# Moving the large tiles and the weight rings to SBUF addresses that are multiples of 2048 bytes, in a two-layer streaming encoder

## What is computed

```python
h = rmsnorm(x, norm_mix[l])
p = h @ w_in[l]                                   # 2048 -> 4608: q, k, v, pooling and conv inputs
y_b = diff_attention(q, k, v, lam, lam_init, diff_head_gain[l])
y_a = multiscale_pool(a_in, pool_w[l], pool_scale[l])
y_c = conformer_conv(c_in, ...)                   # GLU, causal depthwise conv 31, LayerNorm, swish, pointwise
x = x + jnp.concatenate([y_b, y_a, y_c], axis=-1) @ w_out[l]
h = rmsnorm(x, norm_ffn[l])
gu = h @ w_ffn_in[l]                              # 2048 -> 2 x 5504
g = causal_dwconv(gu[..., :D_FF], ffn_conv_w[l], ffn_conv_b[l])
x = x + (jax.nn.silu(g) * gu[..., D_FF:]) @ w_ffn_out[l]   # 5504 -> 2048
```

## The kernel before

| tile | bytes | start before | start after | before mod 2048 | after mod 2048 |
|---|---|---|---|---|---|
| x | 16384 | 16512 | 40960 | 128 | 0 |
| xg | 32768 | 32896 | 57344 | 128 | 0 |
| raw | 16384 | 65664 | 90112 | 128 | 0 |
| whi | 16384 | 82048 | 106496 | 128 | 0 |
| wlo | 16384 | 98432 | 122880 | 128 | 0 |
| con | 2304 | 114816 | 16512 | 128 | 128 |
| half | 4096 | 125088 | 26784 | 160 | 160 |
| gt | 4128 | 129184 | 30880 | 160 | 160 |
| y | 4096 | 133312 | 35008 | 192 | 192 |
| mix, hidden | 32768, 88064 | 137408 | 139264 | 192 | 0 |
| qT, kT, v | 8192 each | 170176 on | 172032 on | 192 | 0 |
| glu | 4576 | 194752 | 196608 | 192 | 0 |
| pw_sb, E, att and the rest | | 199328 on | 201184 on | 672 | 480 |

## Time and profile before

### The profile page before, as it was taken

The page is one execution under the profiler, slowest core; times in us unless marked ns, Lnnn a source line. Parts: engine busy times, 40 slices in busy tenths (PEclk is TensorE's granted clock), DMA queues, the critical chain, the costliest instruction groups (busy, mean ns, idle before and its releaser), DMA issues.

```text
span 2200.1 us, 35784 instructions
## 1 busy us (share of the span) xinstructions
PE 2109.1 (96%) x11874; PEld 1825.4 (83%) x11874; DVE 1522.1 (69%) x1941; ACT 1072.9 (49%) x1504; POOL 354.9 (16%) x315
## 2 busy tenths in 40 slices
PE   7769999999999999999997799999999999999997
PEld 6658888888888888888885588888888888888886
DVE  7898677766666666555479976876676666655555
ACT  5325754555555554443362366545554555544433
POOL 5692023000000000110119621220000000001110
PEclk9999999999999999999999899999999999999999
DMA  7334455555655565556563344555555555555553
GB/s 250 129 106 155 142 172 183 192 191 179 199 188 188 180 200 189 182 177 208 193 203 116 132 147 134 178 193 191 191 191 191 181 192 190 191 192 191 189 191 136
DMA packets 108534, 391.80 MB, mean 178 GB/s; under 512 B 12176, under 2 KB 12688, under 8 KB 108176
## 3 DMA queue, kind: packets, MB, share of 16 engines
q1 hardware_dynamic: 107136, 386.98, 53.4%
q10 hardware_dynamic: 1296, 3.55, 0.5%
HBM read 388.38 MB, written 2.10 MB: 177 GB/s over the span
## 4 chain that ended last, share of the span: by engine, by line
PE 85%; issue 6%; DVE 6%; POOL 1%; ACT 1%; DVEq 0%; DMA 0%; SPq 0%; POOLq 0%; ACTq 0%
PE bank L1134 54%; PE bank L1135 27%; DVE gt L711 3%; PE bank L1203 2%; DVE wlo L666 1%; PE bank L1192 1%; PE bank L1194 1%; PE bank L1193 1%; POOL ssq L1038 0%; POOL sq L1035 0%; PE bank L1253 0%; ACT whi L374 0%; DMA x<-xT 0%; DVE x L1013 0%; DVE x L875 0%
## 5 line engine op out<-in xcount | busy, mean ns | idle before, releaser
L666 DVE TENSOR_TENSOR wlo<-raw,whi 128x1024 fp32r<-128x1024 f32 x728 | 945.3, 1306 | 610.8 <-ACT whi L374 609.7
L1134 PE MATMUL bank<-xg,whi 128*128 128x512 f32 x3648 | 1293.7, 399 | 68.0 <-DVE wlo L666 24.8
L374 ACT ACTIVATE whi<-raw 128x1024 fp32r<-128x1024 f32 x728 | 763.5, 1056 | 806.1 <-PE bank L1135 727.7
L1135 PE MATMUL bank<-xg,wlo 128*128 128x256 f32 x3648 | 1025.8, 281 | 0.0
L1134 PEld LDWEIGHTS bank<-xg,whi 128*128 128x128 f32 x3648 | 692.5, 190 | 235.0 <-DVE wlo L666 23.8
L1135 PEld LDWEIGHTS bank<-xg,wlo 128*128 128x128 f32 x3648 | 696.9, 191 | 0.2
L1134 PE MATMUL bank<-hidden,whi 128*128 128x512 f32 x1376 | 484.6, 395 | 0.3
L1135 PE MATMUL bank<-hidden,wlo 128*128 128x256 f32 x1376 | 387.5, 282 | 0.0
L1134 PEld LDWEIGHTS bank<-hidden,whi 128*128 128x128 f32 x1376 | 258.8, 188 | 62.9 <-DVE wlo L666 1.6
L1135 PEld LDWEIGHTS bank<-hidden,wlo 128*128 128x128 f32 x1376 | 258.5, 188 | 0.0
L1134 PE MATMUL bank<-mix,whi 128*128 128x512 f32 x512 | 182.3, 398 | 0.4 <-DVE mix L837 0.4
(11 more groups left out here) (144 smaller groups left out, 1115.5 us busy)
## 6 DMA issues: line engine op xcount, KB each, us to landing
raw<-wstream SPq DMA_DIRECT2D x729, 512.0 KB, 3.4
pw_sb<-pww ACTq DMA_DIRECT2D x2, 1024.0 KB, 5.8
x<-xT SPq DMA_DIRECT2D x3, 512.0 KB, 9.0
outT<-x SPq DMA_DIRECT2D x6, 256.0 KB, 2.1
x<-xT SPq DMA_DIRECT2D x2, 256.0 KB, 4.3
raw<-wstream SPq DMA_DIRECT2D x2, 256.0 KB, 4.5
poolw_sb<-poolw ACTq DMA_DIRECT2D x2, 256.0 KB, 3.7
outT<-x SPq DMA_DIRECT2D x1, 512.0 KB, 3.0
```

Of the source, the lines that this page charges most:

```text
L374: nc.scalar.activation(whi[:, s, :], raw[:, s, :], ACT.Copy).then_inc(hi_ready, 1)
L666: nc.vector.tensor_tensor(wlo[:, s, :], raw[:, s, :], whi[:, s, :], ALU.subtract).then_inc(lo_ready, 1)
L1134: nc.tensor.matmul(ps[bank][:], whi[:, s, blk * P:blk * P + P], mov, start=first, stop=False)
L1135: return nc.tensor.matmul(ps[bank][:, 0:S], wlo[:, s, blk * P:blk * P + P], mov[:, 0:S], start=False, stop=last)
```

## The change

The declarations of the five large tiles move behind the small ones, and a tile of 464 floats that nothing uses fills the gap to the next multiple of 2048. The operations of every engine are the same, in the same order (3389 rows of TensorE's program, 1205 of VectorE's, 814 of ScalarE's, 344 of GpSimd's and 30 of SyncE's before and after): nothing but addresses changes. In the changed file lines stand 4 lower: L1134 becomes L1138.

```diff
+FILLER = 464
 ...
-        x = sb("x", [P, KC, S])
-        xg = sb("xg", [P, KC, 2 * S], f32r)
-        raw = sb("raw", [P, RING, PIECE])
-        whi = sb("whi", [P, RING, PIECE], f32r)
-        wlo = sb("wlo", [P, RING, PIECE], f32r)
         con = sb("con", [P, NCON])
         par = sb("par", [P, NPAR + 1])
 ...
         gt = sb("gt", [P, NT, S + 2])
         y = sb("y", [P, NT, S])
+        sb("filler", [P, FILLER])
+
+        x = sb("x", [P, KC, S])
+        xg = sb("xg", [P, KC, 2 * S], f32r)
+        raw = sb("raw", [P, RING, PIECE])
+        whi = sb("whi", [P, RING, PIECE], f32r)
+        wlo = sb("wlo", [P, RING, PIECE], f32r)

         with ExitStack() as mixers:
             mix = sb("mix", [P, KC, 2 * S], f32r, mixers)
```

## The result

The changed kernel takes 2217.5 us (median of 4, 2209.9 to 2221.5), the kernel before 2200.8 in the same series (4 runs, 2198.72 to 2202.6). The ratio is 1.0074, 95% interval 1.0056 to 1.0091: slower by 0.74%. The forecast was 2195.5, in a range of 2187 to 2203. The profiled execution took 2216.8 us with a span of 2215.0 us, 14.9 us more than the span of before.

What follows compares the result with a forecast made beforehand. TensorE's matmuls were taken to bound the kernel. 3.9 us gained over `hidden` less 0.6 lost in stage C gave 3.3 us: 2195.9 from the median 2199.18, stated as 2195.5, range 2187 to 2203.

Steps and rivals of the forecast that it cites:

- What bounds the kernel: Whole span: TensorE, its matmuls busy 96% of it, sets the time; the last-ending chain runs over TensorE for 85%.
- Pace goes with the distance to the rings: TensorE pairs: distance by 2048 between moving tile and weight rings sets the pace; `xg` at 0, slower `mix` and `hidden` at 64.
- The rival that addresses do nothing: Whole kernel: pace may go with place in SBUF or stage, not remainder; 2199, within 2 us; chance 0.27.
- Pairs over `hidden`: Stage D, 1376 pairs: `hidden` takes `xg`'s two levels; 3.9 us gained, 0.3 at worst, 6.9 at best.
- odds of 7 in 15: Two restarts a layer over `hidden`: odds of the slow level, 0.3533, leaving 3.0 us lost.
- Pairs over `mix`: Stage B, 512 pairs near 0.3533: nothing booked; 1.4 us a layer gained if a long run is drawn fast.
- the 47 pairs behind them: First 47 pairs of stage C in each layer: run on slow behind `mix`, 0.6 us lost.
- The cycles above the column count: 64 of 832 cycles in each pair might vanish: tens of microseconds; chance 0.02 within the 0.13 case without a slow level.
- The float32 matmuls of the earlier trace then reset the level to fast for the 1326 pairs behind them.: Stage C: plain float32 matmuls of 256 columns lead to 0.3467, as in 6 of 6 restarts; no loss booked.
- booked nothing for `xg`: Pairs over `xg`: tile and rings move together, their distance by 2048 stays 0, so 0 us.
- slow level in stage C: Rival: the reset ends at 0.3533, 8.8 us lost a layer; 2205 for one layer, 2214 for both; chance 0.10.

Runs made afterwards that it cites:

- experiment 4: Kernel before with rings moved by 2016 bytes: `xg` 32 bytes off the rings, `mix` 96, `hidden` 128; 2197.2 us, ratio 0.9983.
- experiment 7: Kernel before with small tiles and 1952 bytes put between `xg` and the rings: `xg`, `mix`, `hidden` all at distance 32; 2191.05 us, ratio 0.9947.
- experiment 8: Kernel before with rings moved by 2016 bytes: `xg` 32 bytes off the rings, `mix` 0, `hidden` 160; 2193.28 us, ratio 0.9958.
- experiment 14: Changed kernel with the rings ahead of `x` and `xg`: `xg`, `mix`, `hidden` 32 bytes off the rings, `con` still at 128; 2191.78 us, ratio 0.9956.
- experiment 9: Kernel before with all small tiles 128 bytes higher, large tiles at their old remainders; 2210.03 us, ratio 1.0048.
- experiment 10: Kernel before with `con` alone 128 bytes higher, all other tiles at their old remainders; 2202.79 us, ratio 1.0015.
- experiment 12: Changed kernel with all small tiles 256 bytes from the rings in place of 128; 2200.77 us, ratio 0.9994 against the kernel before.
- experiment 13: Changed kernel with `con` declared behind the other small tiles, at distance 0 from the rings; 2198.74 us, ratio 0.9992 against the kernel before.
- experiment 2: Kernel before with a gap of 1984 bytes putting `mix` and `hidden` at distance 0 from the rings; 2200.29 us, ratio 0.9988.
- experiment 3: Kernel before with a gap of 1984 bytes putting `hidden` alone at distance 0 from the rings; 2201.03 us, ratio 0.9993.
- experiment 5: Changed kernel's order of declarations with the filler 32 floats longer, large tiles at remainder 128 by 2048; 2197.62 us, ratio 0.9981 against the kernel before.
- experiment 6: Kernel before with everything shifted by 1920 bytes, so that `xg` and the rings start on multiples of 2048; 2202.2 us, ratio 1.0001.
- experiment 11: Kernel before with `ssq` and the small tiles behind it 128 bytes higher, `con` and `par` as before; 2200.8 us, ratio 0.9998.
- experiment 1: Changed kernel with `mix` and `hidden` back at distance 64 from the rings; 2218.96 us, ratio 1.007 against the kernel before.

## Why the prediction was wrong

**What bounds the kernel**: right. No engine but TensorE changed its time, and the changes of its pace and clock account for the span to a few tenths of a microsecond.

**Pace goes with the distance to the rings**: right, and shown by experiments 4, 7, 8 and 14, on three tiles and at several places. `hidden` lost its level of 0.3489 as forecast and went on at stage C's pace without a seam. The rival that addresses do nothing fell. The 16-byte lines of the Trainium skill ("SBUF — State Buffer", Specifications), which spoke for it, do not cover this: all large tiles start on multiples of 32 in every kernel here, and 32 bytes between `xg` and the rings still change the pace by up to 1.9% (0.3533 against 0.3467).

**Pairs over `hidden`**, booked at 3.9 us gained: 1.0 us in the profiled execution. The term was mis-sized. The first 195 pairs of each layer continued a stage C that was slow itself, and of the four restarts behind waits two took the slow level. Over all six kernels with `hidden` at 0 the restarts that I gave odds of 7 in 15 for it took it in 17 of 24.

**Pairs over `mix`**, booked at nothing, and the 47 pairs behind them, booked at 0.6 us lost: right; both long runs over `mix` were slow and the 47 pairs with them.

**The cycles above the column count** (64 of 832 in each pair) were priced too low in a rival: at 2.4 GHz they are 0.0267 us a pair, 148 us for the 5536 pairs, not tens. The forecast does not use it.

**The step that failed**: "The float32 matmuls of the earlier trace rows then reset the level to fast for the 1326 pairs behind them." I had counted 6 of 6 fast restarts and carried them over to other addresses, and booked nothing for `xg` because its distance to the rings stays. But the change also moves the small tiles, `con` with them, from 0 to 128 bytes off the large ones (modulo 256), which my table of addresses showed and the argument left out. With `con` at 128 the restart behind the ssq matmuls was slow in both layers: 17.7 us. Experiments 9 and 10 bring the effect into the kernel before, and 12 and 13 take it out of the changed one, each by moving small tiles only. In the profiled executions with `xg` at distance 0, stage C was fast in all 16 openings where `con` was at 0 or 256 (before, experiments 2, 3, 5, 6, 11, 12, 13), and slow in 6 of 8 where it was at 128 (the change, experiments 1, 9, 10). The rival with this outcome ("slow level in stage C", both layers, 2214) had a chance of 0.10 and named the place and the price, 8.8 us a layer, correctly.

The 6 restarts were also not of one kind. Only two of them stood behind matmuls over `ssq`; the other four stood behind those over `sq`, with the same ones of `con` in the array, and over `gt`. These four are fast in the changed kernel as well. One over `sq`, its first pair at full pace and the last of its run:

```profile
220.61 0.59 PE L1207 MATMUL bank<-sq,con 128*128 128x256 f32 x2
...
221.39 0.40 PE L1138 MATMUL bank<-xg,whi 128*128 128x512 f32 x1
...
223.47 0.40 PE L1138 MATMUL bank<-xg,whi 128*128 128x512 f32 x1
```

Six steps in 2.08 us are 0.3467. In the four kernels with `con` at 128 and `xg` at 0 all 8 restarts behind `sq` were fast, so `con` at 128 does not slow every restart behind float32 matmuls. What sets the one behind `ssq` apart is open.

What else is not settled: `con` alone was enough in 3 of 10 executions in the old layout, all small tiles in 7 of 7. In the changed layout 9 of the 10 executions of the change and of experiment 1 took 2209.9 us or more; the tenth took 2205.09, which the time alone does not place, since experiment 6 had one of 2205.67 with both stages C fast. With `con` put back all 11 took 2203.06 or less. So the slow stage C of the changed layout needs `con`'s distance, but how often it comes depends on more than that distance; the other small tiles may have a part that they do not have alone (experiment 11). In experiment 9 the float32 matmuls followed 47 pairs at 0.3467 in both layers and led once to each level; I found no state ahead of them that decides. Also open are what in the chip the two levels are, and why 128 differs from 0 and from 160.

## What to carry to other kernels

When a chain of matmuls without waits has two rates at one granted clock, count starts over long stretches by operand tile, and try to put the tile that streams and the tile that stands still at a distance where only the fast rate exists; here 32 bytes were worth 0.5%, and a round address was worth nothing. A layout change moves every tile against every other: list the distances of the small ones as well, above all of those that feed the few matmuls ahead of a long stretch, since what is drawn at its start is paid to its end. A frequency counted in one layout is no evidence for another.

## What the runs showed of the hardware that I had not expected

A pair of 512 and 256 columns takes 832 cycles at the granted clock 1.00 at best and 848 in the slow rhythm (0.3533 us); the rhythm, once entered, held for 1326 pairs and 468 us, whatever VectorE, ScalarE and the DMA did meanwhile. In the changed layout the place of `con`, the tile that stands still in two float32 matmuls of 0.24 us together, decided over the 8.8 us that a slow stage C costs behind them. The spread of execution times goes with the levels left to be drawn: 2209.9 to 2221.5 for the changed kernel, 2188.77 to 2191.95 where every tile is at 32.
